# A streaming-encoder layer: two units between convolution and scores, B and C a group early, a convolution in one piece

## What is computed

```
x = x + 1/2 * SwiGLU_1(RMSNorm(x))
u = RMSNorm(x); P = u @ w_in    # -> lru_x | lru_gate | ssd_z | ssd_xBC | ssd_dt | gate logits
A = (GeLU(lru_gate) * RG_LRU(conv4(lru_x))) @ w_br_lru
y = SSD_scan(silu(conv4(x|B|C)), dt) + D*x ; B' = RMSNorm_by_group(y * silu(z)) @ w_br_ssd
x = x + (sigmoid(gA) * A + sigmoid(gB) * B') @ w_out
x = x + 1/2 * SwiGLU_2(RMSNorm(x)) ; final RMSNorm
```

## Time and profile before

| | us |
|---|---|
| median of 3 runs | 2059.88 (2058.93 to 2061.96) |
| the profiled execution | 2059.99 |
| its span | 2058.4 |
| TensorE busy | 1913.9 (93%) |
| VectorE busy | 1173.5 (57%) |
| ScalarE busy | 599.5 (29%) |
| GpSimd busy | 187.6 (9%) |
| granted clock of TensorE, mean | 0.964 |

### The profile page before, as it was taken

One profiled execution on the slowest core, in us unless ns is written; L12 is line 12 of the kernel. 1 busy time (PEld: TensorE's weight loads), 2 busy tenths in 40 slices (PEclk: granted clock), 3 DMA queues, 4 the chain that ended last, 5 costly groups with the idle time before them and its releaser, 6 DMA issues.

```text
span 2058.4 us, 31668 instructions
## 1 busy us (share of the span) xinstructions
PE 1913.9 (93%) x12827; PEld 1856.7 (90%) x12827; DVE 1173.5 (57%) x1524; ACT 599.5 (29%) x786; POOL 187.6 (9%) x273
## 2 busy tenths in 40 slices
PE   7999999997999799897997989798889999999997
PEld 7999999997999799797987888787789999999996
DVE  5442442445688755647668786787645442442444
ACT  4331221223576312132214123211333221221222
POOL 0000000000021211102212211220000000000000
PEclk9999999998999999998999999899989999999998
DMA  4222222223222323341233224123522222222222
GB/s 124 71 81 72 72 79 74 72 69 117 57 71 67 98 75 85 101 119 57 67 110 98 57 72 121 57 70 101 199 85 82 77 76 71 75 78 71 73 68 74
DMA packets 270349, 172.18 MB, mean 84 GB/s; under 512 B 8638, under 2 KB 261814, under 8 KB 269961
## 3 DMA queue, kind: packets, MB, share of 16 engines
q1 hardware_dynamic: 239792, 129.52, 22.1%
q0 software_dynamic: 6576, 26.26, 4.3%
q10 hardware_dynamic: 23900, 15.28, 2.4%
HBM read 150.54 MB, written 20.48 MB: 83 GB/s over the span
## 4 chain that ended last, share of the span: by engine, by line
PE 77%; DVE 13%; issue 5%; ACT 4%; ACTq 1%; DVEq 0%
PE pu L588 69%; DVE xf L1224 3%; ACT w_hi L896 2%; PE pn L818 1%; DVE w_lo L1230 1%; PE pn L767 1%; PE pn L783 1%; DVE lmat L1574 1%; PE pn L787 1%; DVE squares L1526 1%; PE pn L757 1%; DVE xf L1387 1%; DVE xc L1224 0%; PE pu L830 0%; DVE xf L1386 0%
## 5 line engine op out<-in xcount | busy, mean ns | idle before, releaser
L1230 DVE TENSOR_TENSOR w_lo<-w_raw,w_hi 128x1024 fp32r<-128x1024 f32 x241 | 295.2, 1225 | 654.3 <-ACT w_hi L896 652.4
L588 PE MATMUL pu<-act_hi,w_hi 128*128 128x320 f32 x2352 | 546.0, 314 | 23.2 <-DVE h_t L1612 10.3
L588 PE MATMUL pu<-act_lo,w_hi 128*128 128x320 f32 x2352 | 540.7, 311 | 2.1 <-DVE act_lo L1269 2.1
L588 PE MATMUL pu<-act_hi,w_lo 128*128 128x320 f32 x2352 | 540.0, 311 | 0.0
L896 ACT ACTIVATE w_hi<-w_raw 128x1024 fp32r<-128x1024 f32 x241 | 254.8, 1057 | 859.8 <-PE pu L588 857.5
L588 PEld LDWEIGHTS pu<-act_hi,w_hi 128*128 128x128 f32 x2352 | 398.8, 190 | 35.6 <-issue 27.4
L588 PEld LDWEIGHTS pu<-act_lo,w_hi 128*128 128x128 f32 x2352 | 396.9, 190 | 3.6 <-DVE act_lo L1269 3.1
L588 PEld LDWEIGHTS pu<-act_hi,w_lo 128*128 128x128 f32 x2352 | 397.5, 190 | 0.0
L588 PE MATMUL pu<-h_hi,w_hi 128*128 128x320 f32 x1056 | 241.0, 309 | 0.7 <-DVE ff_g L1286 0.7
L588 PE MATMUL pu<-h_hi,w_lo 128*128 128x320 f32 x1056 | 240.6, 309 | 0.0
L588 PE MATMUL pu<-h_lo,w_hi 128*128 128x320 f32 x1056 | 240.6, 309 | 0.0
(11 more groups left out here) (284 smaller groups left out, 1974.3 us busy)
## 6 DMA issues: line engine op xcount, KB each, us to landing
w_raw<-in_ffn_w_up_dram SPq DMA_DIRECT2D x88, 512.0 KB, 3.8
w_raw<-in_w_in_dram SPq DMA_DIRECT2D x73, 512.0 KB, 3.9
w_raw<-in_ffn_w_down_dram SPq DMA_DIRECT2D x32, 512.0 KB, 3.8
w_raw<-in_w_br_ssd_dram SPq DMA_DIRECT2D x16, 512.0 KB, 4.1
w_raw<-in_ffn_w_down_dram SPq DMA_DIRECT2D x16, 384.0 KB, 3.3
es<-e_spill POOLq DMA_DIRECT2D x40, 128.0 KB, 4.1
merged<-gate_spill POOLq DMA_DIRECT2D x8, 640.0 KB, 4.2
h_a<-in_state_ssd_h_dram POOLq DMA_DIRECT2D x8, 512.0 KB, 6.2
```

The lines of the kernel that those rows point to most:

```text
L588: ins = pe.matmul(dst[:, h, :], w[:, side, c, :], a[:, k, h * HALF:(h + 1) * HALF], start=(at == 0), stop=(at == n - 1))
L1230: dve.tensor_tensor(w_lo[:, side, :, :], w_raw[:, side, :, :], w_hi[:, side, :, :].bitcast(F32), ALU.subtract).then_inc(s["w_lo_done"], 1)
```

## The change

- The mixer's order comes from one table, `FILL`. B and C of group g+1 (`xb(g+1,4)`, `xb(g+1,5)`) are computed in group g, into a buffer of their own (`bc`). Between the last `xb` of a group and `scores(0)` stand `z(g,0)` and a branch unit (in group 0 `bl(0)`, in group 3 `z` alone); the units beside and behind each tile move up one place.
- ScalarE takes the last unit behind a tile only after the next tile's exponential (`held`). VectorE has the functions `begin` and `finish` for such a split, but its `held` stays empty: it does both halves of a branch unit ahead of the next `scores`.
- `ext` is laid out as 40 blocks of 3 + 16 columns. ScalarE fills it with three copies and writes `w[3]*x + bias` with a fourth instruction; VectorE adds the three other taps over all 640 tokens.
- At tile 4 the z products and squares come before the `old_states` copies, and the unit beside tile 4 stands ahead of `old_states(0)` on TensorE.
- Gate values have a buffer `gbuf`; `y_t` is dropped, `outputs` works in `es`.
- Group 3's branch input is scaled by its rstd before the split, so `branch_out` adds PSUM straight to `acc_ssd`; the last norm sum stands ahead of `gs(7)`; the last two merge copies of ScalarE are spread between the tail copies.
- At the start: x is loaded before the first weight, which is loaded and cut in four parts; the first unit's products run k-tile by k-tile; the 19 parameter loads move from ScalarE's queue to SP's; FFN 1's first norm sum comes after the first unit.

```diff
+FILL = {0: ([("z", 0, 0), ("bl", 0)],
+            [[("z", 0, 1)], [("z", 0, 2)], [("z", 0, 3)], [("gl", 4)]],
+            [[("gl", 1), ("bl", 1)], [("gl", 2), ("bl", 2)], [("gl", 3), ("bl", 3)], [("bl", 4), ("gl", 5)]],
+            [("bl", 5)], [("xb", 1, 4)], [("gl", 6), ("bl", 6), ("xb", 1, 5), ("gl", 7), ("bl", 7)]),
+        3: ([("z", 3, 0)],
+            [[("z", 3, 1)], [("z", 3, 2)], [("z", 3, 3)], [("br", 2, 3)]],
+            [[("br", 2, 0)], [("br", 2, 1)], [("br", 2, 2)], [("gs", 4)]],
+            [("gs", 5)], [], [])}
+for g in (1, 2):
+    FILL[g] = ([("z", g, 0), ("br", g - 1, 0)],
+               [[("z", g, 1)], [("z", g, 2)], [("z", g, 3)], [("gs", 2 * g - 2)]],
+               [[("br", g - 1, 1)], [("br", g - 1, 2)], [("br", g - 1, 3)], [("xb", g + 1, 4)]],
+               [("gs", 2 * g - 1)], [("xb", g + 1, 5)], [])
...
@@ SP @@
-            load(0, 0, 2, 0, cols(ffn1_w_up[0], 0))
             for t in range(NT):
...
+            for c in range(4):
+                sp.dma_start(w_raw[:, 0, 2 * c:2 * c + 2, :], cols(ffn1_w_up[0], 0, 2 * c, 2)).then_inc(
+                    s[f"w_part{c}" if c < 3 else "w_in0"], 16)
             load(1, 0, 2, 0, cols(ffn1_w_up[0], FFN))
...
+            for src, t, r in rows:
+                sp.dma_start(vec_rows[r:r + src.shape[0], t, :], src).then_inc(s["params"], 16)
...
@@ GpSimd @@
+                    if t > 1:
+                        pool.wait_ge(s["ssd_v"], g * SV_GRP + SV * (t - 2) + SV_Y)
...
@@ TensorE @@
+                fill(before)
                 for t in range(NT - 1):
                     scores(t)
-                    mix_unit(("z", g, t), act_hi, act_lo)
+                    fill(beside[t])
                     inner(t)
...
-                    if g == 0:
-                        lru_branch_unit(t)
-                        mix_unit(("gl", t + 1), act_hi, act_lo)
-                    else:
-                        branch_unit(g - 1, t)
+                    fill(behind[t])
...
                 scores(NT - 1)
+                fill(sampled_unit)
                 old_states(0)
-                if g == 0:
-                    lru_branch_unit(4)
-                else:
-                    mix_unit(("gs", 2 * g - 2), act_hi, act_lo)
                 inner(NT - 1)
+                fill(middle)
                 from_states(0)
...
@@ ScalarE @@
-                act.activation(ext[:, HIST:HIST + HALF], pu[o % 2][:, 0, 0:HALF], ACT.Copy).then_inc(s["ext_in"], 1)
-                act.activation(ext[:, HIST + HALF:EXT_P], pu[o % 2][:, 1, 0:SEQ - HALF], ACT.Copy).then_inc(s["ext_in"], 1)
...
+                act.activation(ext[:, :, HIST:BLOCK].rearrange("p (h b) c -> p h b c", h=2), pair, ACT.Copy).then_inc(s["ext_in"], 1)
+                act.activation(ext[:, 1:half + 1, 0:HIST], pair[:, 0, :, DEC_L - HIST:DEC_L], ACT.Copy).then_inc(s["ext_in"], 1)
...
+                act.activation(halves(dst), pu[o % 2][:, :, 0:HALF], ACT.Identity, scale=v(w), bias=v(bias)).then_inc(s["ext_in"], 1)
...
+                fill(before[:1])
+                held = before[1:]
                 for t in range(NT):
...
                     act.activation(lmat[:, :, :].rearrange("p (b h) l -> p b (h l)", b=2), pn[1][:, :, :],
                                    ACT.Exp).then_inc(s["ssd_a"], 1)
+                    fill(held)
                     if t < NT - 1:
-                        silu_z(g, t)
...
+                        fill(beside[t] + behind[t][:-1])
+                        held = behind[t][-1:]
...
             for r in range(4):
-                take_mix(("br", GROUPS - 1, r), 1)
-                for m in range(2):
-                    merged_split(2 * r + m)
-            for a in range(TAIL_OUTS):
+                branch(GROUPS - 1, r)
+                if r < 3:
+                    merged_split(2 * r)
+                    merged_split(2 * r + 1)
+            for a in range(TAIL_OUTS):
+                if a in (1, 3):
+                    merged_split(6 + a // 2)
+                tail_out(a)
...
@@ VectorE @@
+                for k in (2, 1, 0):
+                    ins = stt(blocks, ext[:, :, k:k + DEC_L], v(w + step * k), blocks, ALU.mult, ALU.add)
...
+                else:
+                    dve.wait_ge(s["br_s"], n - KT + 1)
+                    dve.tensor_tensor(halves(acc), halves(acc), out(o), ALU.add).then_inc(s["out_free"], 1)
...
+                held = []
+                fill(before)
                 for t in range(NT - 1):
                     scores(t)
-                    silu_z(g, t)
+                    for name in held:
+                        finish(name)
+                    fill(beside[t])
                     outputs(t)
...
+                    fill(behind[t])
+                    held = []
...
                 scores(NT - 1)
-                old_states(0)
-                decay_in(NT - 1)
-                decay_states(0)
                 sv(NT - 2, SV_Y)
...
+                fill(sampled_unit)
+                old_states(0)
+                decay_in(NT - 1)
+                decay_states(0)
+                fill(middle)
                 old_states(1)
...
             ssd_gate(6)
+            norm_scale(GROUPS + 1, 0.25 / 512)
+            dve.wait_ge(s["rs_step"], 4 * (GROUPS + 1) + 4)
             ssd_gate(7)
-            norm_scale(GROUPS + 1, 0.25 / 512, squares[:, 1, :])
...
```

More of the change, by code:

```diff
@@ L94 @@
 TAIL_OUTS = 5
+XB_AT = {name: n for n, name in enumerate(name for name in U_AT if name[0] == "xb")}
 V_SCW, V_SCB, V_LCB = 0, 96, 120
@@ L628, in last_sum, with first_unit @@
                 norm_sum(SQ_FFN2 + KT)
+            def first_unit():
+                open_out(O_FFN1)
+                dst = out(O_FFN1)
+                for k in range(KT):
+                    if k % 2 == 0:
+                        pe.wait_ge(s["w_part_lo"] if k < 6 else s["w_lo_done"], k // 2 + 1 if k < 6 else 1)
+                    for w, a, name in ((w_hi, act_hi, "xh_done"), (w_lo, act_hi, None), (w_hi, act_lo, "xl_done")):
+                        if name:
+                            pe.wait_ge(s[name], XH_FFN1 + k + 1)
+                        for h in range(2):
+                            ins = pe.matmul(dst[:, h, :], w[:, 0, k, :], a[:, k, h * HALF:(h + 1) * HALF],
+                                            start=(k == 0 and a is act_hi and w is w_hi), stop=(k == KT - 1 and a is act_lo))
+                ins.then_inc(s["out_ready"], 1)
             def first_rows():
@@ L769, in inner @@
                     ins.then_inc(s["ssd_p"], 1)
-                for k in range(PAIRS + 2):
+                before, beside, behind, sampled_unit, middle, after = FILL[g]
+                for k in range(PAIRS):
                     mix_unit(("xb", g, k), act_hi, act_lo)
@@ L970, in _, with cut_part @@
-            assert len(rows) + 7 == N_PARAMS
-            cut_weights(0, 2, 0)
+            act.dma_start(g1_rows[:, :], norm_ffn1_g[0].rearrange("(k p) -> k p", p=P)).then_inc(s["g1_in"], 16)
+            def cut_part(c):
+                act.wait_ge(s[f"w_part{c}" if c < 3 else "w_in0"], 16)
+                act.activation(w_hi[:, 0, 2 * c:2 * c + 2, :], w_raw[:, 0, 2 * c:2 * c + 2, :], ACT.Copy).then_inc(
+                    s["w_part_hi" if c < 3 else "w_hi_done"], 1)
+            act.wait_ge(s["conv"], 1)
@@ L1115, in _, with branch, fill @@
+            def branch(g, r):
+                take_mix(("br", g, r), 1)
+            def fill(names):
+                for name in names:
+                    {"z": silu_z, "br": branch, "gl": lru_gate, "bl": lru_branch, "gs": ssd_gate, "xb": xbc}[name[0]](*name[1:])
             lru_gate(0)
             lru_split(KT - 1)
+            xbc(0, 4)
+            xbc(0, 5)
             for g in range(GROUPS):
[L1118 to L1128 removed]
+                before, beside, behind, sampled_unit, middle, after = FILL[g]
+                for k in range(PAIRS):
+                    xbc(g, k)
@@ L1369, in _ @@
             for k in range(KT):
+                if k % 2 == 0:
+                    c = k // 2
+                    dve.wait_ge(s["w_part_hi"] if c < 3 else s["w_hi_done"], c + 1 if c < 3 else 1)
+                    part = slice(2 * c, 2 * c + 2)
+                    dve.tensor_tensor(w_lo[:, 0, part, :], w_raw[:, 0, part, :], w_hi[:, 0, part, :].bitcast(F32),
+                                      ALU.subtract).then_inc(s["w_part_lo"] if c < 3 else s["w_lo_done"], 1)
                 dve.wait_ge(s["xh_done"], XH_FFN1 + k + 1)
@@ L1528, in branch_out, with branch, xbc, fill @@
                     dve.tensor_tensor(acc, acc, br_t, ALU.add).then_inc(s["br_s"], 1)
+                else:
+                    dve.wait_ge(s["br_s"], n - KT + 1)
+                    dve.tensor_tensor(halves(acc), halves(acc), out(o), ALU.add).then_inc(s["out_free"], 1)
+            def branch(g, r):
+                for m in range(2):
+                    branch_out(g, r, m)
+            def xbc(g, k):
+                name = ("xb", g, k)
```

(11 more changed lines are left out.)

423 lines of the change are left out of this document (212 added, 211 removed).

## The result

The changed kernel takes 2119.61 us (median of 4 runs, 2115.69 to 2121.78) against 2060.92, a ratio of 1.0284 (95% interval 1.0267 to 1.0301): 58.7 us slower, where +31 was forecast and the range ended at 2110. Its profiled execution is one of 2121.78 us with a span of 2120.2, 61.8 more than the span of before.

A forecast was written before the change was run, and what follows sets the result against it. The prediction took TensorE as the bound everywhere, with losses in the mixer's three middle groups and the merge. Terms -34.5 + 56.6 + 24.3 - 10 - 4.5 - 0.5 = +31.4 on 2059.99 gave 2091 us, range 2031 to 2110.

The forecast's parts named there:

- The steps: Tile steps of the four groups: late `w_hi` lets GpSimd hold VectorE's cut, `inner` waits for `lmat`; +56.6 us (0 to +75).
- Rival B: Steps: the cut is not held up by GpSimd, so the added waits are gone; 2034 us, chance 0.18.
- Rival C: Steps: the cut gets in between GpSimd's two multiplies, 33 us less; 2058 us, no change, chance 0.08.
- The clock in the steps: TensorE's clock falls behind the steps' waits for `lmat`, costing 1.5 us each (range 0 to 2.6).
- Rival D: TensorE's clock stays high in gaps of 2.8 to 3.6 us; 2066 us, chance 0.10.
- `scores(0)`: Start of each group's tiles: `scores(0)` comes earlier, its wait for the last convolution shrinking; -34.5 us (-49.6 to 0).
- Rival F: The change does not do what it says: `scores(0)` waits as before; 2125 us, chance 0.05.
- The sampled tile: Tile 4 to next group: TensorE idles for the gate unit's buffer, then runs C at low clock; +24.3 us (0 to +35).
- Rival E: Tile 4 costs nothing more, as TensorE finds cover; 2067 us, chance 0.09.
- The start: Kernel start: earlier row loads, moved parameter DMAs and a first cut in four let the second unit start earlier; -4.5 us.
- The merge: Merge behind the groups: fewer `acc_ssd` instructions and earlier tail transposes, against later `yn_lo` and gates (+3.5); net -10 us.
- The LRU stage: LRU stage: pace set by gates, tanh, `g_t` and the units; -0.5 us (-3 to +3).

The follow-up runs named there:

- e3_nomask: Changed kernel with GpSimd's mask multiplies for tiles 1 to 4 cut to 4 of 128 columns per head (outputs not the layer's); 2042.1 us, 0.9918 of before.
- e2_unheld: Changed kernel with ScalarE taking every unit at once, none held until the next exponential, VectorE as changed; 2042.2 us, 0.9899 of the kernel before.
- e1_split: Changed kernel with VectorE splitting a branch unit as ScalarE does, second half with its cut behind `lmat`; 2046.6 us, 0.9929 of the kernel before.
- e4_gate_first: Changed kernel with the unit beside tile 4 taken by ScalarE and VectorE right behind `lmat`; 2117.8 us, 1.0266 of the kernel before.
- e7_c_late: e1_split with C of the next group (in group 0 B) moved behind the state part; 2035.7 us, 0.9873 of the kernel before.

## Why the direction was right and the size too small

**The steps: right.** Forecast +56.6, measured +57.1, for the reason given (by group the errors are larger, and cancel: in group 0 I had not allowed for a first step that was slow already, 27.2 us for 25.8, and in group 3 I had priced too little). Rival B (the cut not held up) and C (it gets between GpSimd's multiplies) are excluded by the 4.37 us cut, which ends 1.1 us behind GpSimd's second multiply. e3_nomask shows that GpSimd does it, e2_unheld that ScalarE's hold brings the cut into its way, e1_split that the cost is `lmat`'s place behind it. Rival C goes with the rule of the Trainium skill (SBUF — State Buffer, on the shared port pair) that the instruction that starts first holds the pair. e1_split speaks against it a second time: `lmat` began 0.46 us first and was the one held. The taps at tile 0, above, behave as the rule says, so it holds for some instructions of this kernel and not for others, and my sentence that a VectorE instruction with both inputs in SBUF does not advance while GpSimd multiplies was too wide.

**The clock in the steps: right.** I took 1.5 us for each fall. Group 1 has a natural test: one step, from 1030.11 to 1051.62, had the same 2.69 us wait and a granted clock of 1.00 throughout, and took 21.51 us; those with the fall (0.93) took 23.1. That is 1.6. Rival D (no fall) is out as a rule: it came true in two of the fourteen steps that waited, this one and the second of group 0 (28.55 us for 30.2).

**`scores(0)`: right.** -10.9 in group 0 for -10.6, a wait of 5.3 us in group 3 for the 5.7 forecast. From a group's start it comes 49.2, 50.2 and (one unit added) 49.5 us later in groups 1 to 3, for the 49.1, 49.1 and 48.8 forecast and 56.9 before: some 2 us of the 22.8 are here. Rival F is out.

**The sampled tile: the mechanism right, a size wrong, and this is the larger part of the miss.** The idle time of 12.0 us for the 10.9 forecast came with its place and cause as told. The failed step is the one from there to the next group: I let the low clock hit the C unit (9.7 us) and took the rest at the speed of before. The C unit took only 7.5 us in group 1 and 7.3 in group 2, and the state part, which I had left at its old price, went from 15.5 to 23.0. In groups 1 to 3 the state parts grew by 3.9, 7.5 and 6.3 us; in group 0, where before two units stood in its middle and its two pieces took 17.6, by 5.4. Together 23 us. Measured from tile 4 to the next group's start, the term came to +9.7, +11.4, +14.1 and +8.8 us by group (0 to 3) for the +3.9, +10.0, +8.8 and +1.6 forecast. So +24.3 came to some +44, beyond its upper bound of +35: the state parts gave 23 us, and the two C units took back 4.6. With the start it carried the time past the end of the range. Rival E (this costs nothing) is out.

What puts the clock down there is only partly settled. The length of the idle time ahead alone does not decide it (e4_gate_first: 5.6 us for 12.0, the same 0.56; e3_nomask: 12.0, and 18.7 us). Taking B or C out from ahead of it and restoring the order at tile 4 together bring it back to 16 us; what each does alone is within the scatter, save the 16.7 us of e7_c_late in group 2. Which of the waits decides, or whether the short products themselves do, isn't shown.

**The start: wrong, by 8.9 us.** The failed step is "19 issues of some 0.4 us, behind `w_raw`, ahead of the third weight load; they end well before VectorE frees that side". The issues did (the last at 17.9). I had counted issues where the landing counts: the last two DMAs hold 2048 packets, and moved to the end of the SP queue they were issued 8 us later than in the kernel before (16.5 for 8.5). What TensorE gained on the second unit (6.2 us) it lost in the wait behind it. The trace of before had shown it: for some 9 us its DMA engines move next to no bytes, and the third weight, issued at 14.65, lands at 35.8. The prediction has no term for it, and its bounds for the start (-7 to 0) leave it out.

**The merge: right** (-11.7, or -10.9 with the norm sum set aside, for -10): the adds are gone, and the wait of 8.5 us at the tail transposes is down to 1.0; against that stands a new one of 5.5 for `yn_hi`, in the place where +3.5 was forecast. The LRU stage is right too (-0.2 for -0.5).

## What to carry to other kernels

Where a queue is moved or an instruction held back, ask for the first instruction behind it that shares a resource with another engine, and follow what is queued behind that one: here a cut of 1.2 us whose input comes 3.7 us late costs 57 us over the steps of four groups. Ask of every DMA in a start-up queue how many packets it is, not how many bytes or issues. And where a stretch of the kernel before is already granted less than the full clock (0.90 and 0.91 between tile 4 and the next `scores(0)`), price the whole stage at the low clock for the upper bound, the parts that the change doesn't touch as well.
